# Keys, values and key Grams of the prompt on the other partition half, small PE products written in alternating pairs, and the turn's order rewritten

## The reference, cut

```
proj = rmsnorm(x) @ w_in
conv_out = silu(layernorm(depthwise_conv(glu(proj))))      # 512 channels, width 31
r, k, v, w, kk, a, g = token shift and small products of proj  # 8 heads of 64
S = S * w[:, None, :] + (S @ -kk)[:, None] * (kk * a) + v[:, None] * k   # for each token
y = S @ r
x = x + concat(conv_out, (groupnorm(y) + bonus) * g) @ w_out
x = x + hierarchical_moe(rmsnorm(x))                       # top 2 of 32 experts
```

## Time and profile before

| | us |
|---|---|
| median of 3 runs (1158.47 to 1163.6) | 1159.81 |
| profiled execution | 1162.31 |
| its span | 1160.5 |
| PE busy | 1101.3 (95%) |
| DVE busy | 665.4 (57%) |
| ACT busy | 365.8 (32%) |
| POOL busy | 214.0 (18%) |

### The profile page before, as it was taken

One profiled execution on the slowest core, in us unless ns is written; L12 is line 12 of the kernel. 1 busy time (PEld: TensorE's weight loads), 2 busy tenths in 40 slices (PEclk: granted clock), 3 DMA queues, 4 the chain that ended last, 5 costly groups with the idle time before them and its releaser, 6 DMA issues.

```text
span 1160.5 us, 24234 instructions
## 1 busy us (share of the span) xinstructions
PE 1101.3 (95%) x9392; PEld 666.0 (57%) x9393; DVE 665.4 (57%) x1154; ACT 365.8 (32%) x720; POOL 214.0 (18%) x278
## 2 busy tenths in 40 slices
PE   7999999999998799999989999967999999999986
PEld 5666666666666688999984555534333333333342
DVE  6288999993554687888744232365343343433416
ACT  6000011011322657777641211022223232232324
POOL 4000000010001113332320001001233233333200
PEclk9999999999998899999999999977999999999999
DMA  9211111010000111111233321057998889999739
GB/s 270 79 36 37 37 37 37 27 43 23 1 1 8 19 20 24 23 20 22 54 136 99 105 73 51 31 225 285 380 348 330 301 329 342 419 406 403 317 125 389
DMA packets 97791, 171.45 MB, mean 148 GB/s; under 512 B 44490, under 2 KB 69249, under 8 KB 88419
## 3 DMA queue, kind: packets, MB, share of 16 engines
q1 hardware_dynamic: 90211, 152.31, 36.8%
q0 software_dynamic: 7488, 17.84, 4.4%
HBM read 153.64 MB, written 25.91 MB: 155 GB/s over the span
## 4 chain that ended last, share of the span: by engine, by line
PE 82%; DMA 6%; DVE 5%; SPq 3%; ACT 2%; issue 1%; POOLq 0%; DVEq 0%; ACTq 0%
PE ps L1655 27%; PE ps L2120 14%; PE ps L1970 10%; PE ps L2150 8%; PE ps L1667 7%; PE ps L1688 3%; PE ps L2107 2%; DMA arena<-y_rows 2%; PE ps L1676 1%; PE ps L2000 1%; DMA arena<-in_w_exp_down_dram 1%; SPq L537 1%; PE ps L2136 1%; DMA late<-in_w_gate_up_dram 1%; PE ps L1985 1%
## 5 line engine op out<-in xcount | busy, mean ns | idle before, releaser
L1655 PE MATMUL ps<-arena 128*128 128x384 f32 (+1 forms) x1032 | 316.6, 468 | 0.0
L1655 PEld LDWEIGHTS ps<-arena 128*128 128x128 f32 x1032 | 195.3, 190 | 118.0 <-issue 1.9
L2120 PE MATMUL ps<-arena 128*64 x416 | 188.5, 596 | 4.1 <-DVE arena L2860 1.7
L2123 PE MATMUL ps<-arena 128*64 128x512 f32 x416 | 188.5, 596 | 0.0
L2272 DVE SCALAR_TENSOR_TENSOR arena<-arena,cw 128x1024 f32<-128x1024 f32 x240 | 168.2, 778 | 0.4
L2120 PEld LDWEIGHTS ps<-arena 128*64 128x64 f32 x416 | 54.5, 136 | 112.6 <-issue 112.5
L1970 PE MATMUL ps<-arena 128*128 128x512 f32 x256 | 113.1, 596 | 0.0
L1667 PE MATMUL ps<-arena 64*64 64x64 f32 x2960 | 97.5, 219 | 5.0 <-DVE arena L2606 1.6
L2150 PE MATMUL ps<-arena 128*64 x208 | 96.5, 607 | 2.4 <-ACT arena L1412 2.4
L2153 PE MATMUL ps<-arena 128*64 128x512 f32 x208 | 96.5, 607 | 0.0
L1667 PEld LDWEIGHTS ps<-arena 64*64 64x64 f32 x2960 | 92.0, 135 | 7.2 <-issue 4.8
(11 more groups left out here) (368 smaller groups left out, 1527.5 us busy)
## 6 DMA issues: line engine op xcount, KB each, us to landing
arena<-in_w_exp_gate_dram SPq DMA_DIRECT2D x32, 1024.0 KB
arena<-in_w_exp_up_dram SPq DMA_DIRECT2D x32, 1024.0 KB
arena<-in_w_exp_down_dram SPq DMA_DIRECT2D x32, 1024.0 KB, 10.4
arena<-in_w_in_dram SPq DMA_DIRECT2D x22, 512.0 KB, 4.0
arena<-in_x_prompt_dram SPq DMA_DIRECT2D x16, 512.0 KB, 7.8
arena<-y_rows SPq DMA_DIRECT2D x8, 1024.0 KB, 17.0
arena<-in_w_out_dram SPq DMA_DIRECT2D x2, 2048.0 KB
xn_rows<-arena SPq DMA_DIRECT2D x8, 512.0 KB, 2.8
```

What stands on the lines that cost most here:

```text
L1655: ins = pe.matmul(banks(proj_bank(q) + piece)[:, 0:n1 - n0], win[q % 6][:, c, :], xnT[:, c, n0:n1], start=(c == 0), stop=(c == DC - 1))
L2120: pe.matmul(banks(b)[0:HS, :], xgT[b][:, c, 0:HS], wring_gu[:, bass.ds(slot, 1), 0:2, c, :].rearrange("p a w f -> p (a w) f"), start=(c == ...
L2123: ins = pe.matmul(banks(b)[HS:P, :], xgT[b][:, c, HS:P], wgu[b][:, :, c, :], start=(c == 0), stop=(c == DC - 1))
```

## The change

- `product`, `token` and `gram_of` issue one head pair; `half=other` puts result (tokens, Grams) or operands (keys, values) on the half opposite to the head. vtok, ktok and the key Gram `GK` of the eight prompt tiles now lie there. The sample tile stays as it was.
- PE's turn is rewritten: pairs of different halves alternate (`gram_and_values`, `key_tokens`, key Gram inside `level_x(4)`, keys' part of rhs, state and output inside other products). Chain steps take banks 6 and 7 in turn.
- ACT's and DVE's turns are written in a new order.
- The convolution's layer norm is done in three pieces (512, 512 and 64 tokens): pieces 0 and 1 at the end of the projection and in turn 0, piece 2 in the last turns.

```diff
...
+        def key_bank(j):
+            return 6 if j < 2 else 1
+        def tok_bank(j):
+            return 6 if j else 1
+        def chain_bank(n, product):
+            return 7 if (product + n) % 2 == 0 else 6
+        B_RHS, B_U, B_S = 0, 1, 0
...
+            def turn(j):
                 i = j - 1
                 if j >= 3:
                     gn_root(j - 3)
-                if j < NT - 1:
-                    decay_tanh(j + 1)
+                if j == 3:
+                    conv_root(2)
+                norms_wide(j + 1)
                 tok_copy(j, 0, vtok, 0)
-                if j < NT - 1:
-                    iclr_tanh(j + 1)
-                else:
-                    powers_copy(0)
-                if j:
-                    rhs_copy(2 * i)
-                    x_copies(i, 4)
-                tok_copy(j, 1, btok, 1)
-                if j < NT - 1:
-                    norms_wide(j + 1)
-                if j == NT - 1:
-                    powers_copy(1)
-                if j:
-                    conv_tanh(i)
+                iclr_tanh(j + 1)
+                rhs_copy(2 * i)
+                x_copies(i, 4)
+                decay_tanh(j + 1)
+                tok_copy(j, 1, btok, tok_bank(j))
                 tok_copy(j, 2, ktok, 0)
-                if j:
-                    x_copies(i, 5)
-                    u_copy(2 * i)
-                if j == NT - 1:
-                    powers_copy(2)
+                x_copies(i, 5)
+                u_copy(2 * i)
                 if j >= 3:
-                    gn_affine(j - 3, 1)
-                if j == NT - 1:
-                    state_in(0)
-                elif j:
-                    blocks_turned(j)
-                else:
-                    exps(1)
-                    blocks_turned(0)
-                if j:
-                    y_copy(i, 0, 2)
-                if j == NT - 1:
-                    state_in(1)
-                if j:
-                    rhs_copy(2 * i + 1)
-                if 0 < j < NT - 1:
-                    exps(j + 1)
-                if j:
-                    u_copy(2 * i + 1)
-                if j == NT - 1:
-                    state_in(2)
-                    state_in(3)
+                    gn_affine(j - 3, 4)
+                rhs_copy(2 * i + 1)
+                y_copy(i, 0, 2)
+                exps(j + 1)
+                key_scale(j + 1)
+                u_copy(2 * i + 1)
+                blocks_turned(j)
                 if j >= 2:
                     gn_square(j - 2)
-                if j < NT - 1:
-                    key_scale(j + 1)
-                if j:
-                    y_copy(i, 1, 3)
+                y_copy(i, 1, 3)
...
+            def same(p):
+                return slice(p, p + 64)
+            def other(p):
+                return slice(64 - p, P - p)
+            def product(hp, dst, lhs, rhs, first=True, last=True, alone=False, half=same):
+                for p in (0, 64):
+                    h, k = slice(p, p + 64), half(p)
+                    ins = pe.matmul(dst[h, hp * 64:hp * 64 + 64], lhs[k, hp, :], rhs[k, hp, :],
+                                    start=alone or (first and hp == 0), stop=alone or last, skip_group_check=True)
+                return ins
...
+            def token(hp, c, b, src, half):
+                for p in (0, 64):
+                    h = slice(p, p + 64)
+                    ins = pe.matmul(banks(b)[half(p), (c * CT + hp) * 64:(c * CT + hp + 1) * 64],
+                                    src[h, hp, c * 64:c * 64 + 64], ident[h, h], start=True, stop=True)
+                return ins
...
+            def gram_of(hp, j, c, lhs, half):
+                t = slice(c * 64, c * 64 + 64)
+                for p in (0, 64):
+                    h = slice(p, p + 64)
+                    ins = pe.matmul(banks(2 + c)[half(p), hp * P:(hp + 1) * P], lhs[h, hp, t],
+                                    AR[j % 3][h, hp, :, t], start=True, stop=True)
+                return ins
...
+            def gram_and_values(j):
+                for c in range(2):
+                    if j >= 2:
+                        pe.wait_ge(y_done, 2 * j - 3 + c)
+                    for hp in range(CT):
+                        first_gram = gram_of(hp, j, c, bt, same)
+                        value = token(hp, c, 0, values(j), other)
+                first_gram.then_inc(gb_psum, 1)
+                value.then_inc(tok_psum, 1)
+            def key_tokens(j):
+                for c in range(2):
+                    for hp in range(CT):
+                        b_token = token(hp, c, tok_bank(j), bt, same)
+                        k_token = token(hp, c, 0, kt, other)
+                b_token.then_inc(tok_psum, 1)
+                k_token.then_inc(tok_psum, 1)
...
+            def first_u(i):
+                n = 2 * i
                 pe.wait_ge(rhs_done, n + 1)
-                if c == 0:
-                    pe.wait_ge(x_done, level_count(i, 5, 1))
-                heads(banks(7)[:, 0:256], XF[:, c, :, :], RHS, alone=True).then_inc(u_psum, 1)
-            def chain_s(i, c):
-                n = 2 * i + c
+                pe.wait_ge(x_done, level_count(i, 5, 1))
+                pe.wait_ge(gk_done, i + 2)
+                for hp in range(CT):
+                    y_keys(i, 0, hp)
+                    ins = solve_u(i, 0, hp)
+                ins.then_inc(u_psum, 1)
+            def first_state(i):
+                n = 2 * i
                 pe.wait_ge(u_done, n + 1)
-                heads(banks(7)[:, 0:256], ktok[i % 2][:, c, :, :], vtok[i % 2][:, c, :, :], last=False)
-                heads(banks(7)[:, 0:256], btok[i % 2][:, c, :, :], UU, first=False).then_inc(s_psum, 1)
-            def chain_y(i, c):
-                n = 2 * i + c
-                t = slice(c * 64, c * 64 + 64)
-                pe.wait_ge(gk_done, i + 2)
-                dst = banks(2 + c)[:, 0:256]
-                heads(dst, AR[i % 3][:, :, 1, t], SS[n % 2], last=False)
-                heads(dst, GK[i % 2][:, c, :, 1, :], vtok[i % 2][:, c, :, :], first=False, last=False)
-                heads(dst, GB1[i % 2][:, c, :, :], UU, first=False).then_inc(y_psum, 1)
+                for hp in range(CT):
+                    rhs_keys(i, 1, hp)
+                    ins = state_u(i, 0, hp)
+                ins.then_inc(s_psum, 1)
+                for hp in range(CT):
+                    y_keys(i, 1, hp)
+                    y_state(i, 0, hp)
+                for hp in range(CT):
+                    ins = y_u(i, 0, hp)
+                ins.then_inc(y_psum, 1)
+            def second_rhs(i):
+                pe.wait_ge(s_done, 2 * i + 2)
+                for hp in range(CT):
+                    ins = rhs_state(i, 1, hp)
+                ins.then_inc(rhs_psum, 1)
+            def second_u(i):
+                pe.wait_ge(rhs_done, 2 * i + 2)
+                for hp in range(CT):
+                    state_keys(i, 1, hp)
+                    ins = solve_u(i, 1, hp)
+                ins.then_inc(u_psum, 1)
+            def second_state(i):
+                for hp in range(CT):
+                    y_state(i, 1, hp)
+                pe.wait_ge(u_done, 2 * i + 2)
+                for hp in range(CT):
+                    ins = state_u(i, 1, hp)
+                ins.then_inc(s_psum, 1)
+                for hp in range(CT):
+                    ins = y_u(i, 1, hp)
+                ins.then_inc(y_psum, 1)
...
+            def turn(j):
+                i = j - 1
+                n = 2 * i
+                scaled_ready(j)
+                gram_and_values(j)
+                pe.wait_ge(kk_done, 2 * j + 1)
+                pe.wait_ge(s_sum, n)
+                decay(j + 1, decay_bank(j + 1))
+                iclr(j + 1)
                 if j == 1:
                     pe.wait_ge(cvar_done, len(PIECES))
-                if j:
-                    chain_rhs(i, 0)
-                    level_x(i, 4)
-                if j:
-                    pe.wait_ge(decay_sum, min(j + 2, NT))
-                    to_tokens(j, 1, bt)
-                if j == NT - 1:
-                    sample_inverse(1)
+                if j >= 2:
+                    pe.wait_ge(rk_used, j - 1)
+                if j >= 4:
+                    pe.wait_ge(mix_done, j - 3)
+                free_for_rhs(i, 0)
+                for c in range(2):
+                    x = level_in(i, 4, c)
+                    for hp in range(CT):
+                        if c == 0:
+                            rhs_keys(i, 0, hp)
+                        ins = product(hp, banks(4 + c)[:, 0:256], PT[i % 2][:, c, :, :], x, alone=True)
+                    ins.then_inc(yl_psum, 1)
+                pe.wait_ge(yl_psum, level_count(i, 4, 0))
+                pe.wait_ge(s_done, n + 1)
+                for hp in range(CT):
+                    ins = rhs_state(i, 0, hp)
+                ins.then_inc(rhs_psum, 1)
+                pe.wait_ge(prod2_done, j + 1)
+                pe.wait_ge(gb_done, j + 1)
```

(88 more changed lines are left out.)

397 lines of the change are left out of this document (224 added, 173 removed).

## The result

The change takes 1180.78 us (median of 4 runs, 1179.27 to 1184.61) against 1161.70 of the kernel before in the same series: 1.0174 times, 95% interval 1.0146 to 1.0202. It is slower by some 19 to 20 us; the forecast was 1175, range 1156 to 1206. The profiled execution of after took 1184.61 (span 1182.8, PE's mean granted clock 0.959), the slowest of its four; that of before took 1162.31.

What follows compares the result with a forecast made beforehand. PE's queue was taken as the bound, the inverse's loop through DRAM as second. Turns +1, half clock +16.8, ends -0.8 and -1.5 summed to +15.5 us: 1177.8 for the profiled execution, 1175 for the median, range 1156 to 1206.

Steps and rivals of the forecast that it cites:

- the loop through `blocks_turned` behind `exps` and `key_scale`: Block inverse through DRAM back to PE: `blocks_turned` waits on ACT behind both, 6.7 us where 3.5 would be.
- one thing that it took for a cost: DVE's order: `keys` ahead of `small_blocks`, put down as 1.83 us more on the loop each turn.
- What bounds the kernel: Prompt turns before the change: PE's queue sets the pace; the loop of 22.5 us is second, with 2.8 slack.
- Step 1, the pairs: PE's products on four quadrants at once: 6.4 of 25.5 us saved a turn, PE's own work down to 19.1.
- Rival A: PE's issue limit of 26.7 ns a record holds for the whole array: +2.2 us a turn, 1191; chance 0.22.
- Rival B: The paired halves on PE do not overlap: loop 30.2 us, time 1206; chance 0.08.
- Step 2, the loop: Level product to level product through PE, DVE, ACT and DMA: 25.6 us a turn against 25.46, +1 over seven turns.
- Step 3, the clock: PE idles 5 us a turn, then restarts at half clock: 2.4 us at each of seven restarts, +16.8.
- rival C: PE's granted clock stays full in spite of the gaps: 1158.5, no change; chance 0.12.
- Step 4, the ends: Outside the repeated turns: -0.8 for values beside the first Gram, -1.5 for the last prompt turn.
- Step 5, the layer norm: Convolution's norm in three pieces, moved to where DVE has idle time: cost 0, at most 1.4 us.
- Rival D: Same loop but shorter, through faster `key_scale` and issues, at full clock: turn 24.8 us, time 1153; chance 0.15.

Runs made afterwards that it cites:

- run 7: The change with `blocks_turned` ahead of the second `rhs_copy`, DVE order `small_blocks`, `whole_blocks`, `new_state`, `keys`, and `bonus` behind `cumulate`: 1181.08 us.
- run 5: The change with keys, values and key Gram on the same half as their head: 1210.45 us, 1.0409 times the kernel before.
- run 3: The change with three extra, unused 128x512 products on PE behind `iclr` in turns 2 to 7, in the gap: 1180.09 us.
- run 4: The change with `bonus` moved on PE behind `second_rhs` and `cumulate`: 1176.43 us, 1.0127 times the kernel before.
- run 9: The change with `cumulate` directly behind `first_u`, `blocks_turned` directly behind `exps`, and `new_state(0)` behind `whole_blocks`: 1154.55 us, 0.9926 times the kernel before.
- run 1: The change with `blocks_turned` ahead of the second `rhs_copy` on ACT: 1168.13 us, 1.0045 times the kernel before.
- run 6: The change with `blocks_turned` ahead of the second `rhs_copy` on ACT and `keys` behind `whole_blocks` on DVE: 1182.17 us.
- run 8: As run 7, but with keys, values and key Gram on the same half as their head: 1184.74 us.
- run 11: As run 9, but with keys, values and key Gram on the same half as their head: 1174.75 us.

## Why the prediction was right, and where it was not

The direction, the size and the cause named first (the loop through `blocks_turned` behind `exps` and `key_scale`) hold; the sizes of two terms were wrong and in part cancelled, which is luck, and one thing that it took for a cost was a necessity. Against the profiled execution, for which the sum was made, it had +15.5 where 22.3 was measured: 3.3 of the 6.8 are missing in the seven turns, 3.5 at the ends.

*What bounds the kernel.* That PE bound the turn of before and the loop was second stands in the traces. A third bound, the ring through the first transfers, was not seen, nor that the change adds `keys` to it by the new wait of `cumulate`. The trace of before had only a weak sign of it. In four of the seven turns `small_blocks` starts 7.75 us behind the first mask, as at 478.91 in the earlier trace rows, directly behind the last mask and without a wait; in the other three it waits for the landing of the first transfers, 1.3 us in all:

```profile
DVE arena L2450 <- DMA arena<-u_blocks: 1.3, 3, 0.7
```

In run 7 it waits for it in all seven turns, 1.0 to 3.7 us each.

*Step 1, the pairs.* Four quarters run side by side: 0.95 for the tokens where 0.93 was written. **Rival A** (issue limit of 26.7 ns) is out. The section "Wait — 56ns, not 53.3ns?" of "TensorE: Matmul & The Clock Gate" in the Trainium skill says that starts never come closer than about 25 ns. By measurement that holds on two quarters (29.1) and not on four (14.8 on average). (The 1189 that the prediction worked out from it sums to 1188.) **Rival B** (no overlap) has its price in run 5: 1210, against the 1206 written. PE's busy time fell by 4.0 us a turn; the 6.4 of the prediction counts starts and not busy time, and part of it came back as the stalls below.

*Step 2, the loop.* In the prediction's own terms, for one turn:

| leg | predicted | after |
|---|---|---|
| landing to `keys`, clock full | 6.0 | 7.1 (run 3, the five restarts at full clock) |
| `keys` to `small_blocks` | 1.83 | 1.77 |
| `small_blocks` to the end of `blocks_turned` | 9.26 | 10.11 |
| to the landing | 8.5 | 8.39 |
| half clock, mean of the seven turns | 2.4 | 1.2 (8.3 less 7.1) |
| turn | 28.0 | 28.5 |

The sum without the clock was 1.8 us too short. 0.85 of it is `bonus` and a stall ahead of `second_rhs` (run 4 gives 0.76 of the turn back); the 1.1 of the first leg is in part PE stalls: in the turn at full clock of the change, at 392.07, the leg is 6.74, and one stall among the token products takes 0.5 of the 0.74 that this is above 6.0. The rest is not split further.

*Step 3, the clock.* It fell at each restart as forecast, and **rival C** is out, but the price was the term that was mis-sized: 2.4 a turn predicted, 1.4 measured at a restart by run 3's trace, 1.2 as the mean of the seven turns. Two things made it too large. The spell of half clock lasts 3.1 to 5.9 us behind the restart, 4.1 on average, where the prediction took the 5.2 and 5.7 of the earlier trace rows. And not all of it reaches the loop: at the four restarts compared in run 3 the spells of the change last 4.6 us on average, which could cost half of that, 2.3, and cost 1.4, so 0.9 is hidden where the prediction's "some hides the hand-offs" had 0.3. I have no run that shows which of the work in a spell lies off the loop.

*Step 4, the ends.* The first level product starts at 392.07, 1.9 us earlier than before (0.8 forecast). The last prompt turn with the sample tile, from its level product to the output projection, takes 44.8 us where it took 42.0: +2.8, and -1.5 was forecast. The clock is half from 589.8 to 596.6 there, and PE waits 2.45 us for four masked copies on DVE (L2788) that stand behind the second `new_state`; in the kernel before the same wait is 1.64, so it is 0.8 of the 2.8:

```profile
615.48 0.42 DVE L2677 TENSOR_TENSOR arena<-arena 128x256 f32<-128x256 f32 x1
615.82 0.68 DVE L2692 TENSOR_REDUCE arena<-arena 128x8 f32<-128x512 f32 x1
616.42 2.49 DVE L2788 TENSOR_TENSOR arena<-arena,late 128x512 f32<-128x512 f32 x4
```

This was not tried by itself. The sum closes: -1.9, +21.1 for seven turns, +2.8, and 0.3 behind it give the 22.3 us between the two spans.

*Step 5, the layer norm.* DVE's busy time is 665.6 us against 665.4, and the loop starts earlier. No cost showed; it was not tested by itself.

**Rival D** (faster through a shorter loop) was wrong for this kernel. Run 9 comes close to its numbers, a turn of 24.93 and 1154.6 us where D had 24.8 and 1153, but by another cause than D's faster `key_scale`, so it does not bear D out. It is nearer to the prediction's remark that without the wait for `cumulate` the loop would be 3.2 us shorter, 22.4; the turn did not come down that far, nor the time to 1140 (by the prediction's own terms 1136).

## What to carry to other kernels

Before costing an edit, trace every ring that closes within one turn, not only the longest wait: here two rings share DVE and ACT, and each move that shortened one (runs 1, 6, 7) lengthened the other, until the step that both needed (`cumulate`) was taken from behind the chain. A faster engine gives what it has on the ring that holds: the pairs are worth 29.7 us in the change's order (run 5), 3.7 in that of run 7 (run 8) and 20 in that of run 9 (run 11). A buffer that moves to another bank can bring a new wait, and the wait can close a ring: look for it in the diff before trusting the old kernel's slack. An operation that looks idle in front of a critical one may be there to keep another ring open.

## What the runs showed of the hardware

**Four quarters, and then the instruction supply.** The row "issue" in PE's waits can stand for a wait that the profile does not ascribe (the 24.8 us of `cumulate` in run 6 end 0.1 us behind `keys` in every turn) or for a stall with no wait in front. In run 9 one of them falls in the middle of 64 token products between which no wait is written:

```profile
470.06 0.57 PE L1716 MATMUL ps<-ident,arena 64*64 64x64 f32 x23
471.80 0.75 PE L1716 MATMUL ps<-ident,arena 64*64 64x64 f32 x36 [1.18 <-issue]
```

I numbered all instructions of PE's queue in each trace (weight loads, products and the sequencer's own, in order of start, from 0) and listed each distance of more than 0.33 us between the starts of two products in the seven turns where the later one carries no wait (`decay`, `iclr` and extra products left out). In these kernels the pause ends at the same remainder, 193, of the number divided by 256, in all but eight cases, two in run 1, one in run 9 and five in run 8, which are 0.34 to 0.37 us where products of another shape begin or have just begun; they are left out of the table. In run 3 the extra products shift which product has that number, and the stalls go with the number:

| kernel | stalls at 193 mod 256, in the seven turns | of blocks of 256 | us in all |
|---|---|---|---|
| before, 8, 11 (two quarters) | 0 | 35 to 36 | 0 |
| after | 8 | 35 to 36 | 7.3 |
| 1 | 13 | 35 to 36 | 11.1 |
| 3 | 11 | 35 to 36 | 9.3 |
| 9 | 13 | 35 to 36 | 13.3 |

So every 256 instructions PE can stop for 0.4 to 1.9 us, and in the seven turns it does so only in kernels whose pairs use four quarters. Outside them it is not only these. In the sample tile, among products on two quarters, the kernel before has one such stall, at remainder 193 too:

```profile
608.05 0.73 PE L1920 MATMUL ps<-arena 64*64 64x64 f32 x17 [1.51 <-issue]
```

and so have after (629.90) and run 11 (622.99). The section "Instruction fetch mechanics" of "Runtime: NRT & Kernel Launch" in the Trainium skill says that instructions are fetched in blocks of 256 and that crossing from one to the next is mostly hidden. The count of 256 agrees with it; that the stalls are these fetches is an inference from it, and no run here shows the fetch itself. Nothing showed of them in 35 to 36 blocks of the turns at 29 ns a record, and 13.3 us in those of run 9, where pairs run at 14.8. That is PE's time; how much of it run 9's own time would lose without them is not shown.

**The granted clock** was at half behind each of the seven gaps of 4.0 to 6.5 us in front of a level product of the change. With 2.7 us of products put into six of them, 0.4 to 2.6 us of gap were left, and four of the six restarts were at full clock; the other two, behind 2.15 and 2.59 us, were not, though two behind 2.34 and 2.49 were (run 3).
